# Column slabs outside the feed-forwards: one 512-column product for both parts of the activations, the bank's halves summed by VectorE

## What is computed

```
layer 0:  x += mixer_ab(x)          gated recurrence and pooling, input projection 1024 -> 2560
          x += cross_attn(x, mem)   4 heads of 256: q = norm(x) wq, k = norm(mem) wk, v = norm(mem) wv
          x += conv_ffn(x)          gelu(conv(h[:3072])) * h[3072:], h = norm(x) w_up
layer 1:  x += conformer_conv(x)    norm(x) w1 (to 2048), glu, conv of 31 taps, layer norm, silu, w2
          x += cross_attn(x, mem)
          x += conv_ffn(x)
then      x = rms_norm(x)
          h = norm(x) w_in          (dilated q, k, v; sliding q, k, v; two gates of 1024)
          x += (gate1 * dilated_attention + gate2 * sliding_attention) w_out
          x += hier_moe(norm(x))    32 experts of 512, 2 per token
          out = norm(x)
```

## Time and profile before

| | |
|---|---|
| time, median of 3 runs | 1674.98 us (1674.19 to 1675.51) |
| the profiled execution, span of its core | 1674.9 us |
| PE busy | 97% of the span |
| DVE busy | 50% |
| ACT busy | 36% |
| POOL busy | 28% |
| HBM read | 394.02 MB |

### The profile page before, as it was taken

The page is one execution under the profiler, slowest core; times in us unless marked ns, Lnnn a source line. Parts: engine busy times, 40 slices in busy tenths (PEclk is TensorE's granted clock), DMA queues, the critical chain, the costliest instruction groups (busy, mean ns, idle before and its releaser), DMA issues.

```text
span 1674.9 us, 28612 instructions
## 1 busy us (share of the span) xinstructions
PE 1628.1 (97%) x11476; PEld 1290.0 (77%) x11476; DVE 830.0 (50%) x1320; ACT 601.2 (36%) x1019; POOL 471.2 (28%) x257
## 2 busy tenths in 40 slices
PE   7999999999999999999999999999999999999996
PEld 6898998999999699899999998888944444444332
DVE  2665457888875174688887433768711010110102
ACT  2371454444453264444345333656311111111101
POOL 1332424555543142355555443222200000000000
PEclk9999999999999999999999999999999999999999
DMA  7464634555559453455552665262899999999995
GB/s 296 151 218 157 211 114 139 184 180 176 182 183 262 165 165 116 136 188 176 179 185 90 209 217 176 89 229 87 319 394 421 421 422 421 421 422 420 421 421 220
DMA packets 86055, 401.21 MB, mean 240 GB/s; under 512 B 9536, under 2 KB 14272, under 8 KB 61248
## 3 DMA queue, kind: packets, MB, share of 16 engines
q1 hardware_dynamic: 84944, 395.81, 64.5%
q10 hardware_dynamic: 1008, 3.96, 0.6%
HBM read 394.02 MB, written 1.05 MB: 236 GB/s over the span
## 4 chain that ended last, share of the span: by engine, by line
PE 42%; issue 30%; DVE 22%; ACT 4%; POOL 1%; DVEq 1%; DMA 0%; ACTq 0%; SPq 0%; POOLq 0%
DVE wl L1259 6%; DVE cf L1576 5%; PE pw L2064 5%; PE pw L2066 5%; PE pw L2065 5%; PE pw L2377 4%; DVE hid L1592 4%; ACT wh L733 3%; DVE cf L1579 3%; PE acc L2070 2%; PE acc L2064 2%; PE acc L2065 2%; PE acc L2066 2%; PE acc L2236 2%; DVE gpad L1570 1%
## 5 line engine op out<-in xcount | busy, mean ns | idle before, releaser
L1142 POOL TENSOR_TENSOR wl<-raw,wh 128x1024 fp32r<-128x1024 f32 x157 | 387.4, 2468 | 569.4 <-ACT wh L733 565.7
L733 ACT ACTIVATE wh<-raw 128x1024 fp32r<-128x1024 f32 x314 | 325.1, 1051 | 230.8 <-PE pw L2066 104.9
L2064 PE MATMUL pw<-ah,wh 128*128 128x256 f32 x1272 | 364.5, 287 | 5.0 <-POOL wl L1142 3.4
L2065 PE MATMUL pw<-ah,wl 128*128 128x256 f32 x1272 | 359.8, 283 | 0.0
L2066 PE MATMUL pw<-al,wh 128*128 128x256 f32 x1272 | 359.8, 283 | 0.0
L1259 DVE TENSOR_TENSOR wl<-raw,wh 128x1024 fp32r<-128x1024 f32 x157 | 200.9, 1280 | 117.2 <-ACT wh L733 117.0
L2064 PEld LDWEIGHTS pw<-ah,wh 128*128 128x128 f32 x1272 | 243.7, 192 | 10.4 <-issue 6.3
L2065 PEld LDWEIGHTS pw<-ah,wl 128*128 128x128 f32 x1272 | 243.9, 192 | 0.1
L2066 PEld LDWEIGHTS pw<-al,wh 128*128 128x128 f32 x1272 | 243.8, 192 | 0.0
L2064 PE MATMUL acc<-yh,wh 128*128 128x256 f32 x672 | 194.0, 289 | 2.0 <-POOL yl L1211 1.2
L2065 PE MATMUL acc<-yh,wl 128*128 128x256 f32 x672 | 190.1, 283 | 0.0
(11 more groups left out here) (335 smaller groups left out, 2569.2 us busy)
## 6 DMA issues: line engine op xcount, KB each, us to landing
raw<-in_stream SPq DMA_DIRECT2D x358, 512.0 KB, 3.5
raw<-in_experts SPq DMA_DIRECT2D x65, 1024.0 KB, 24.3
ring_w<-in_experts SPq DMA_DIRECT2D x40, 1024.0 KB, 24.3
ring_y<-in_experts SPq DMA_DIRECT2D x30, 1024.0 KB, 23.0
early_e<-in_experts SPq DMA_DIRECT2D x22, 1024.0 KB, 20.8
ring_q<-in_experts SPq DMA_DIRECT2D x11, 1024.0 KB, 21.9
ring_k<-in_experts SPq DMA_DIRECT2D x11, 1024.0 KB, 22.7
ring_a<-in_experts SPq DMA_DIRECT2D x11, 1024.0 KB, 23.4
```

The costliest lines, as they stand in the source:

```text
L733: A.done(act.activation(wh[:, s.base % SPLIT, :], raw[:, slot_of(s.base), :], ACT.Copy), w_hi)
L1142: G.done(pool.tensor_tensor(wl[:, s.base % SPLIT, :], raw[:, slot_of(s.base), :], wh[:, s.base % SPLIT, :].bitcast(F32), ALU.subtract), w_ ...
L2064: pe.matmul(dst, wh[:, s.base % SPLIT, w], hi, start=start, stop=False, **kw)
L2065: pe.matmul(dst, wl[:, s.base % SPLIT, w], hi, start=False, stop=False, **kw)
```

## The change

`ah` and `al` become the two halves of one tensor `a_pair`, and `mh` and `ml` of `m_pair`; their addresses stay. `tile2` multiplies `wh` once by the pair, 512 columns into the whole bank, and adds `wl` times the high part into the first half. The bank then holds `wh*ah + wl*ah` in its first half and `wh*al` in its second. `col_slab` uses it wherever it is given a pair: in the keys of both layers, in the queries, `pw1` and `win` beyond their first three slabs, in slab 44 of `win`, and in the gate slabs. The feed-forwards (`glu`), the leads and `abin` stay with `tile3` or as they were.

DVE must sum the halves. Where nothing is multiplied (keys), the copy becomes one `tensor_reduce` over a view with the halves as the inner axis (`halves_added`). Elsewhere `halves_scaled` multiplies the second half by `rstd_b` into a buffer in SBUF (`t[1]`, or `low_t` of 1 KB that is new) and the first half by `rstd_b` in place in PSUM, fences, and a `tensor_tensor` adds the two.

```diff
+            def halves_added(bank, dst, sem):
+                V.done(dve.tensor_reduce(dst, bank[:, 0:2 * T].rearrange("p (h t) -> p t h", h=2), AX.X, ALU.add), sem)
+
+            def halves_scaled(bank, low, scale=None):
+                high = bank[:, 0:T]
+                V.fence()
+                for dst, src in ((low, bank[:, T:2 * T]), (high, high)):
+                    if scale is None:
+                        V.done(dve.tensor_tensor(dst, src, rstd_b[:], ALU.mult))
+                    else:
+                        V.done(dve.scalar_tensor_tensor(dst, src, scale, rstd_b[:], ALU.mult, ALU.mult))
+                V.fence()
+                return high
...
             def col_out(name, n, dst, scale=None, by=None, slab=None):
...
                 if by is None:
-                    ins = dve.tensor_copy(dst, b)
-                elif scale is None:
+                    halves_added(pw[u % 4], dst, empty_v)
+                    return
+                if name != "abin" and n >= LEAD:
+                    low = t[1][:] if name == "win" else low_t[:]
+                    ins = dve.tensor_tensor(dst, halves_scaled(pw[u % 4], low, scale), low, ALU.add)
+                    V.done(ins, empty_v)
+                    return
+                if scale is None:
                     ins = dve.tensor_tensor(dst, b, by, ALU.mult)
...
             def slab_out(s, u, dst):
-                V.done(dve.tensor_copy(dst, pw[u % 4][:, 0:T]), empty_v)
+                halves_added(pw[u % 4], dst, empty_v)
...
             def gate_out(m, k):
-                    V.done(dve.tensor_tensor(gt[:, n - 46, :], pw[3][:, 0:T], rstd_b[:], ALU.mult), S("gate_out"))
+                    V.done(dve.tensor_tensor(gt[:, n - 46, :], halves_scaled(pw[3], t[1][:]), t[1][:], ALU.add), S("gate_out"))
...
+            def tile2(bank, s, n, pair, start, stop):
+                w = slice(n * P, n * P + P)
+                pe.matmul(bank[:, 0:2 * T], wh[:, s.base % SPLIT, w], pair, start=start, stop=False,
+                          skip_group_check=True)
+                return pe.matmul(bank[:, 0:T], wl[:, s.base % SPLIT, w], pair[:, 0, :], start=False, stop=stop,
+                                 skip_group_check=True)
...
             def fill(m, k, inside=None):
...
-                            last = tile3(pw[3][:, 0:T], s, k, ah[:, k, :], al[:, k, :], k == 0, k == KC - 1)
+                            last = tile2(pw[3], s, k, a_pair[:, :, k, :], k == 0, k == KC - 1)
```

More of the change, by code:

```diff
@@ L334, in program @@
         x = sb("x_res", "x", 0, [P, KC, T])
-        ah = sb("ah", "ah", 0, [P, KC, T], F32R)
-        al = sb("al", "al", 0, [P, KC, T], F32R)
+        a_pair = sb("a_pair", "ah", 0, [P, 2, KC, T], F32R)
+        ah, al = a_pair[:, 0, :, :], a_pair[:, 1, :, :]
         ax = sb("x_gained", "ah", 0, [P, KC, T])
-        mh = sb("mh", "mh", 0, [P, KC, T], F32R)
-        ml = sb("ml", "ml", 0, [P, KC, T], F32R)
+        m_pair = sb("m_pair", "mh", 0, [P, 2, KC, T], F32R)
+        mh, ml = m_pair[:, 0, :, :], m_pair[:, 1, :, :]
         yh = sb("yh", "yh", 0, [P, 12, T], F32R)
@@ L361, in program @@
         cv = sb("cv", "arena", 34, [P, KC, T])
+        cf = sb("cf", "arena", 27, [P, 2, T])
+        hid = sb("hid", "arena", 31, [P, 2, T])
+        uf = sb("uf", "arena", 29, [P, 2, T])
+        low_t = sb("low_t", "arena", 33, [P, T])
         gpad = sb("gpad", "arena", 24, [P, 2, T + 2])
-        cf = sb("cf", "arena", 27, [P, 2, T])
-        uf = sb("uf", "arena", 29, [P, 2, T])
-        hid = sb("hid", "arena", 31, [P, 2, T])
         q2 = sb("q2", "arena", 0, [P, 20, T])
@@ L477, in program @@
         empty_v, empty_a = S("bank_emptied_vector"), S("bank_emptied_scalar")
+        emptier = {"v": empty_v, "a": empty_a}
         acc_full, acc_out = S("sum_full"), S("sum_taken")
@@ L517, in wait_emptied @@
         def wait_emptied(eng, u):
-            eng.wait_ge(empty_v if USES[u] == "v" else empty_a, emptied(u))
+            eng.wait_ge(emptier[USES[u]], emptied(u))
         def wait_acc(eng, phase, n):
@@ L2095, in drain, with col_slab @@
             def drain(u):
-                for who, sem in (("v", empty_v), ("a", empty_a)):
+                for who, sem in emptier.items():
                     if u and emptied(u - 1, who):
                         pe.wait_ge(sem, emptied(u - 1, who))
-            def col_slab(s, u, hi, lo, wait_n=None, first_ready=None):
+            def col_slab(s, u, pair=None, wait_n=None, first_ready=None):
                 wait_split(pe, s)
@@ L2108, in col_slab, with col_phase @@
                         first_ready(k)
-                    last = tile3(pw[u % 4][:, 0:T], s, k, hi[:, k, :], lo[:, k, :], k == 0, k == KC - 1)
+                    if pair is None:
+                        last = tile3(pw[u % 4][:, 0:T], s, k, ah[:, k, :], al[:, k, :], k == 0, k == KC - 1)
+                    else:
+                        last = tile2(pw[u % 4], s, k, pair[:, :, k, :], k == 0, k == KC - 1)
                 last.then_inc(slab_done, 1)
-            def col_phase(name, n, hi, lo, ready=None, hook=None, straight=None, s_off=0, u_off=0):
+            def col_phase(name, n, pair, ready=None, hook=None, straight=None, s_off=0, u_off=0):
                 s0, u0 = S0[name] + s_off, USE0[name] + u_off
@@ L2119, in col_phase @@
                         wait_emptied(pe, u0 + k - 4)
-                    col_slab(At(s0 + k), u0 + k, hi, lo, None, ready if k == 0 else None)
+                    col_slab(At(s0 + k), u0 + k, pair, None, ready if k == 0 else None)
                     if hook:
@@ L2125, in col_phase @@
                         for j in range(straight, straight + 4):
-                            col_slab(At(s0 + j, 4, i), u0 + j, hi, lo, i * 4 + (v0 + j - 3))
+                            col_slab(At(s0 + j, 4, i), u0 + j, pair, i * 4 + (v0 + j - 3))
             def lead(phase, name, pair):
@@ L2336, in step @@
                         bank_free(j, jj, "g")
-                        col_slab(g, u0 + 2 * j, ah, al)
+                        col_slab(g, u0 + 2 * j)
                         bank_free(j, jj, "u")
                     if j >= 1:
-                        col_slab(g + 1, u0 + 2 * j + 1, ah, al, None, spread_at(name) if j == 1 else None)
+                        col_slab(g + 1, u0 + 2 * j + 1, None, None, spread_at(name) if j == 1 else None)
                     if j >= 2:
@@ L2402, in _ @@
                     wait_emptied(pe, u + 3 + j % 2 - 4)
-                    col_slab(At(k0_slab(j)), u + 3 + j % 2, mh, ml, None,
+                    col_slab(At(k0_slab(j)), u + 3 + j % 2, m_pair, None,
                              None if j else lambda k: pe.wait_ge(S("m_lo"), k + 1))
@@ L2429, in cross_layer @@
                 lead(f"q{l}", f"xa{l}", f"q{l}")
-                col_phase(f"q{l}", 8 - LEAD, ah, al, spread_at(f"xa{l}"), queries_hook(l), 8 - LEAD, LEAD, LEAD)
+                col_phase(f"q{l}", 8 - LEAD, a_pair, spread_at(f"xa{l}"), queries_hook(l), 8 - LEAD, LEAD, LEAD)
                 cross(l)
@@ L2437, in _ @@
             lead("pw1", "c", "pw1")
-            col_phase("pw1", 16 - LEAD, ah, al, spread_at("c"), None, 5, LEAD, LEAD)
-            col_phase("k1", 8, mh, ml, lambda k: pe.wait_ge(S("m_lo"), KC + k + 1))
+            col_phase("pw1", 16 - LEAD, a_pair, spread_at("c"), None, 5, LEAD, LEAD)
+            col_phase("k1", 8, m_pair, lambda k: pe.wait_ge(S("m_lo"), KC + k + 1))
             conv()
@@ L2449, in final_spread @@
                     norm_spread("final")
-            col_phase("win", 32 - LEAD, ah, al, spread_at("mix"), final_spread, 5, LEAD, LEAD)
+            col_phase("win", 32 - LEAD, a_pair, spread_at("mix"), final_spread, 5, LEAD, LEAD)
             for b in range(3):
@@ L2455, in _ @@
             wait_emptied(pe, u - 4)
-            col_slab(s, u, ah, al)
+            col_slab(s, u, a_pair)
             s, u = s + 1, u + 1
```

## The result

The changed kernel took 1688.5 us (median of 4 runs, 1687.46 to 1689.4) where the kernel before took 1675.24 in the same comparison: a ratio of 1.0079, 95% interval 1.0067 to 1.0091. It is slower by some 13 us. The forecast was 1674.0 us with a range up to 1682.5; both were wrong.

The account below looks back on a forecast made before the run. PE, busy 97% of the span, was taken to pace. From 1674.9 us, win -3.2, k1 -0.9, pw1 -1.4, layer 0's keys +0.2, cross-attention +1.1 and attention +3.3 gave -0.9: 1674.0 us, 8-in-10 range 1667.5 to 1682.5.

Parts of the forecast that it names:

- full gain: In pw1, DVE's added work stays hidden behind PE, so 13 slabs save 0.107 us each, 1.4 us.
- cover of 5.5 us: In pw1, PE has three more banks ahead and needs a split only two slabs later, some 5.5 us.
- If that cover is gone, up to 1.4 us a pair: In pw1, the fallback: without cover each of the 6 pairs may lose up to 1.4 us.
- Attention, +3.3: Second half's 16 gate slabs on bank 3: 5.0 us of exposed evacuations and fences less 1.7 saved by PE.
- PE's saving of 0.107 us a slab: In 85 changed slabs, PE takes 2.773 us instead of 2.88; 9.1 us if PE paced everywhere.
- Rival C: A short product behind a long one costs what three short ones do, PE saves nothing: 1683.1 us, chance 0.09.
- rival D: The k slabs' reduction pays by the result, +1.05 us instead of +0.27 for 8 slabs: about 1679 us, chance 0.08.
- the cover in `win` and `k1`: DVE's added work is hidden behind PE there: full gain, -3.2 us in win and -0.9 in k1.
- the extra of cross-attention: Last query slab's evacuation delays the next head's maximum by 0.80 us a layer; +1.1 us together after savings.
- A: Rival: attention's and cross-attention's waits absorb DVE's extra work, all but 1 to 2 of 9.1 us remain: 1667 us, chance 0.14.
- B: Rival: the single gate bank decides, each of 16 evacuations adds its whole 0.80 us: 1681.8 us, chance 0.12.
- I am wrong if: Tests of failure: the projection's pace does not change, or attention's stage grows by more than 6 us.

Follow-up runs that it names:

- pw1_one_more: The kernel before, with one more DVE product of 256 columns and a fence a slab in pw1, PE unchanged: 1675.51 us, ratio 0.9998.
- keys_queries_win: The changed kernel with pw1 and the 16 gate slabs as before, so keys, queries and win alone use the pair: 1675.08 us, ratio 0.9998.
- pw1_split_first: The changed kernel with gate slabs as before; in pw1 DVE splits the weights ahead of the even slab's evacuation: 1673.65 us, ratio 0.9984.
- pw1_as_before: The changed kernel with the 13 slabs of pw1 as before: 1681.15 us, ratio 1.0031.
- long_then_short: As keys_queries_win, but a slab's eight 512-column products come first and its eight 256-column products after them: 1676.39 us, ratio 1.0007.
- gate_two_after: The kernel before, each gate slab with two more DVE products reading no bank, after the operation that frees bank 3: 1680.99 us, ratio 1.0029.

## Why the prediction was wrong

- **`pw1`, "full gain"** is the step that failed: -1.4 us forecast with `k1`'s -0.9, +7.0 measured for both. I counted the two loads rightly (DVE 5.5 us a pair, measured 5.24 without a hold; PE 5.55, measured 5.65) and argued that a later DVE would only shorten the hold. That is what pw1_one_more shows. But I took POOL's start as fixed by PE. So it was before: from 470 to 535 ACT's `wh` waited for PE 16 times, 25.4 us in all; in the changed kernel it did so 3 times, for 4.5 us, and ACT's tanh waited for DVE instead, 31.6 us in seven waits. Once DVE's odd sum is late, ACT's tanh and the `wh` behind it are late, and POOL starts by DVE's clock. And I asked only how long the operation then held would stay held, not which operation DVE would reach next inside POOL's 2.40 us: the split, which PE itself waits for. The "cover of 5.5 us" was a stock, and 7.35 - 5.65 = 1.7 us a pair emptied it at once: PE waited for the first time, 0.99 us, behind the second held split. "If that cover is gone, up to 1.4 us a pair" was near in size, yet neither its condition was checked nor was it given a chance.
- **Attention, +3.3** had the right mechanism, exposed evacuations of bank 3: PE's waits were 6.8 us at 9 places where 5 to 6 us were forecast. Two terms were mis-sized: DVE's part is 5.8 us and not 5.0, and PE's saving 0.6 at most and not 1.7.
- **PE's saving of 0.107 us a slab** was got in full in `win` of keys_queries_win and pw1_split_first, and half of it (0.053) in the changed kernel: -1.5 us instead of -3.2. Rival C (nothing) is out. The Trainium skill ("TensorE: Matmul & The Clock Gate", section "Back-to-back issue gap") gives N / 2.4 ns plus 2.5 ns as the gap of an isolated product, which by my estimate makes 0.02 us a slab. Every `win` showed more, 0.053 us or above.
- **Right:** the reduction (687 ns; rival D is out), the three operations (0.34 and 0.46 us), the cover in `win` and `k1`, the sign of the extra of cross-attention (+0.8 where +0.4 was forecast in layer 1, +1.2 where +0.9 was for the keys and queries of layer 0; such steps are within what the clock moves in a trace), and a shift of an early stage passing one for one through the loads of the experts.
- **Rivals:** A is out, B's number (1681.8) is near that of pw1_as_before (1681.15), which has attention's loss alone, but its condition, each evacuation adding all of its 0.80, was not met: 16 of them gave 5.8 us and not 12.8. None of the rivals had `pw1` in it.
- **Signs and sums:** of the signs named, "no PE wait in pw1" is the one that caught the miss. The pace of `win` did change, and attention grew by less than 6 us, so neither of the two under "I am wrong if" was met. And A and C reckon with 9.1 us of saving, while the forecast's own terms credit 8.6, because the queries keep 0.5 of their 1.1; C's time by these terms is 1682.6.

## What to carry to other kernels

Before work is added to an engine that shares a port with another, list every operation of it that the other can hold, and ask which of them falls into the other's window when the queue is late, not only which one does today. Where the other's start hangs on this engine through a third (here DVE, ACT, POOL), a collision can be a rate, paid in each turn of the loop, and the banks ahead cover only its first turns. The remedy here was an order and not less work: the operation that can be held goes ahead of the other's start, and those that read PSUM go beside it.

## What was not expected of the hardware

- The same sequence of a 512-column and a 256-column product took 0.3467 us in `win` of some kernels and 0.3533 in others, with the same code in that stage, and 0.353 to 0.357 in the key slabs. The pure sequence took 0.120 us everywhere.
- TensorE's clock fell to 0.50 for 3 to 4 us at places that differ from trace to trace, with work all around: at 1218 in the changed kernel, and in long_then_short at 1039, after an idle time of PE of 0.70 us that stands in keys_queries_win too, where the clock stayed at 1.00. In long_then_short the 16 products of `acc<-k,q` took 2.94 us instead of 1.58.
- DVE's products of two operands in SBUF were held by POOL as its TENSOR_SCALAR is (668 ns in the mean of the 32 in gate_two_after, 424 in the median, the longest 2.63 us), and its reductions never (414 ns, the longest 0.42 us).
